# Modulation products in fewer, larger groups, and their loads spread over three parts of a step

## What is computed

```python
mod = jax.nn.silu(c) @ p['w_ada'] + p['b_ada']          # (9 rows, 9*2048)
sh1, sc1, g1, sh2, sc2, g2, sh3, sc3, g3 = jnp.split(mod, 9, axis=-1)
h = modulate(rmsnorm(x, p['g_ffn1']), sh1, sc1)
x = x + 0.5 * g1[:, None, :] * swiglu(h, p['w_up1'], p['w_down1'])
h = modulate(rmsnorm(x, p['g_mix']), sh2, sc2)
o, new_state = hybrid_mixer(h, ...)
x = x + g2[:, None, :] * o
h = modulate(rmsnorm(x, p['g_ffn2']), sh3, sc3)
x = x + 0.5 * g3[:, None, :] * swiglu(h, p['w_up2'], p['w_down2'])
```

## Time and profile before

| | |
|---|---|
| median of 3 runs | 2197.51 us (2195.69 to 2198.03) |
| the profiled execution's own time | 2197.48 us |
| its span, first to last instruction | 2195.7 us |
| TensorE matmul busy | 2130.8 us, 97% |
| VectorE, ScalarE, GpSimd busy | 55%, 39%, 6% |
| mean DMA rate | 243 GB/s |

### The profile page before, as it was taken

The page is one execution under the profiler, slowest core; times in us unless marked ns, Lnnn a source line. Parts: engine busy times, 40 slices in busy tenths (PEclk is TensorE's granted clock), DMA queues, the critical chain, the costliest instruction groups (busy, mean ns, idle before and its releaser), DMA issues.

```text
span 2195.7 us, 39972 instructions
## 1 busy us (share of the span) xinstructions
PE 2130.8 (97%) x17405; PEld 1975.2 (90%) x17405; DVE 1209.7 (55%) x1664; ACT 856.9 (39%) x1050; POOL 123.6 (6%) x146
## 2 busy tenths in 40 slices
PE   5999999999999999999988999999999999999998
PEld 4888879888989899989988998999999999999998
DVE  4355575444444445577788967444444444445555
ACT  3433333333333333356646534333433333333332
POOL 0000000000000000011675000000000000000000
PEclk9999999999999999999999999999999999999999
DMA  9988885988888887747554574866577777755453
GB/s 356 336 296 296 281 319 201 329 283 294 306 310 306 310 298 277 248 152 216 159 156 147 173 261 146 292 238 211 178 247 275 278 258 259 258 173 172 147 175 115
DMA packets 394270, 534.17 MB, mean 243 GB/s; under 512 B 13032, under 2 KB 358000, under 8 KB 375408
## 3 DMA queue, kind: packets, MB, share of 16 engines
q1 hardware_dynamic: 371792, 519.28, 68.5%
q10 hardware_dynamic: 22303, 12.33, 1.9%
HBM read 524.37 MB, written 7.19 MB: 242 GB/s over the span
## 4 chain that ended last, share of the span: by engine, by line
PE 88%; DVE 7%; DMA 2%; ACT 2%; issue 1%; SPq 1%; ACTq 0%; DVEq 0%
PE main L1631 23%; PE main L1632 22%; PE main L1633 22%; PE b L1554 5%; PE main L1697 4%; PE main L1699 4%; PE main L1698 4%; DVE w_lo L988 2%; PE b L1564 1%; DMA ada<-in_w_ada 1%; PE b L1577 1%; DMA first<-in_w_ada 1%; DVE ntile L1081 1%; SPq L525 1%; ACT w_hi L677 1%
## 5 line engine op out<-in xcount | busy, mean ns | idle before, releaser
L988 DVE TENSOR_TENSOR w_lo<-raw,w_hi 128x1024 fp32r<-128x1024 f32 (+2 forms) x720 | 796.3, 1113 | 890.8 <-ACT w_hi L677 889.4
L677 ACT ACTIVATE w_hi<-raw 128x1024 fp32r<-128x1024 f32 (+2 forms) x720 | 685.1, 956 | 1075.3 <-PE main L1633 914.1
L1631 PE MATMUL main<-h_hi,w_hi 128*128 128x264 f32 x2960 | 853.2, 288 | 13.5 <-DVE w_lo L988 4.5
L1632 PE MATMUL main<-h_lo,w_hi 128*128 128x264 f32 x2960 | 844.2, 285 | 0.0
L1633 PE MATMUL main<-h_hi,w_lo 128*128 128x264 f32 x2960 | 842.9, 285 | 0.0
L1631 PEld LDWEIGHTS main<-h_hi,w_hi 128*128 128x128 f32 x2960 | 559.9, 189 | 40.6 <-issue 17.8
L1632 PEld LDWEIGHTS main<-h_lo,w_hi 128*128 128x128 f32 x2960 | 558.8, 189 | 0.5
L1633 PEld LDWEIGHTS main<-h_hi,w_lo 128*128 128x128 f32 x2960 | 558.3, 189 | 0.0
L1631 PE MATMUL main<-act_hi,w_hi 128*128 128x264 f32 x1408 | 403.1, 286 | 0.0
L1633 PE MATMUL main<-act_hi,w_lo 128*128 128x264 f32 x1408 | 400.4, 284 | 0.0
L1632 PE MATMUL main<-act_lo,w_hi 128*128 128x264 f32 x1408 | 399.9, 284 | 0.0
(11 more groups left out here) (271 smaller groups left out, 996.0 us busy)
## 6 DMA issues: line engine op xcount, KB each, us to landing
raw<-in_w_up SPq DMA_DIRECT2D x132, 1024.0 KB, 5.3
ada<-in_w_ada SPq DMA_DIRECT2D x112, 1024.0 KB, 9.0
raw<-in_w_down SPq DMA_DIRECT2D x96, 768.0 KB, 5.0
raw<-in_w_up SPq DMA_DIRECT2D x88, 512.0 KB, 5.2
raw<-in_w_in SPq DMA_DIRECT2D x36, 1024.0 KB, 5.3
ada<-in_w_ada_f SPq DMA_DIRECT2D x32, 1024.0 KB, 9.0
ada<-in_w_ada SPq DMA_DIRECT2D x56, 512.0 KB, 7.7
raw<-in_w_down SPq DMA_DIRECT2D x32, 512.0 KB, 8.1
```

Source lines behind the costliest of these rows:

```text
L677: A(split_view(w_hi, m, kind), raw_piece(m, kind), ACT.Copy).then_inc(hi_done, 1)
L988: TT(split_view(w_lo, m, kind), raw_piece(m, kind), split_view(w_hi, m, kind).bitcast(F32), ALU.subtract).then_inc(lo_done, 1)
L1631: MM(out, wh, hi[:, k, :], start=k == 0, stop=False)
L1632: MM(out, wh, lo[:, k, :], start=False, stop=False)
```

## The change

Three things are changed. The products are issued in fewer groups: in the units, two behind every other unit and three behind the last unit of a quarter (`group_at`), and from step 11 on always four, at every other step or, from step 16 to 29, at every step. The loads of a step are issued not all behind part 2 but behind parts 0, 1, 1 and 2, except in the mixer. `mod_place` stands ahead of the piece work of part 3, not behind it. With this, `G1` is copied, turned and placed two units later.

```diff
-        for at, counts in ((UPS, (3, 3, 3, 3, 2, 2, 2, 2)), (UPS + DNS, (4,) * UPS), (2 * UPS + DNS, (2,) * 6),
-                           (S_FF2 + 2, (2,) * 6), (S_FF2 + UPS, (2,) * DNS), (S_FF2 + UPS + DNS, (2,) * 8)):
-            for n, count in enumerate(counts):
-                per_step[at + n] = count
+        for at, every, groups in ((UPS + 1, 2, 2), (UPS + DNS - 3, 1, UPS + 3), (2 * UPS + DNS, 2, 3),
+                                  (S_FF2 + 2, 2, 3), (S_FF2 + UPS, 2, 4), (S_FF2 + UPS + DNS, 2, 4)):
+            for n in range(groups):
+                per_step[at + every * n] = 4
...
+        group_at = {UPS * q + i: range(UPS * q + i - 1, UPS * q + i + 1) for q in range(QS) for i in (1, 3, 5, 7)}
+        group_at.update({UPS * q + 10: range(UPS * q + 8, UPS * q + 11) for q in range(QS - 1)})
+        group_at.update({38: range(37, 39), 40: range(39, 40)})
...
-                            if j == 2:
-                                for a in loads_at.get(s, ()):
-                                    if a == G3 * KD:
-                                        sp.wait_ge(h_ready, 3 * KD)
-                                        sp.wait_ge(stored, 16 * (len(OUT_COPIES) + 1))
-                                    ada_load(a)
+                            for a in loads_at.get(s, ()):
+                                if j != (2 if s >= S_XBC and s < S_FF2 else (0, 1, 1, 2)[a % 4]):
+                                    continue
+                                if a == G3 * KD:
+                                    sp.wait_ge(h_ready, 3 * KD)
+                                    sp.wait_ge(stored, 16 * (len(OUT_COPIES) + 1))
+                                ada_load(a)
...
-                if u == 40:
+                if u == 42:
                     ada_copy(G1)
...
-                if u == 41:
+                if u == 43:
                     mod_place(G1)
...
-                            pieces_ahead(s, j, PIECE_KIND[kind], follows)
                             if j == 3 and s in vec_ends:
                                 mod_place(vec_ends[s])
+                            pieces_ahead(s, j, PIECE_KIND[kind], follows)
...
-                if u == 40:
+                if u == 42:
                     ada_turn(G1)
...
-                if u < 40:
-                    stream_product(u)
+                for n in group_at.get(u, ()):
+                    stream_product(n)
```

More of the change, by code:

```diff
@@ L372, in stream @@
             return (q + 1, i) if i < 8 else (None, 3 * q + i - 8)
+        group_at = {UPS * q + i: range(UPS * q + i - 1, UPS * q + i + 1) for q in range(QS) for i in (1, 3, 5, 7)}
+        group_at.update({UPS * q + 10: range(UPS * q + 8, UPS * q + 11) for q in range(QS - 1)})
+        group_at.update({38: range(37, 39), 40: range(39, 40)})
+        assert [n for u in sorted(group_at) for n in group_at[u]] == list(range(40))
         slot_landed, stream_landed = [32] * 4, []
```

## The result

The changed kernel takes 2185.52 us (median of 5 runs, 2184.51 to 2187.82) against 2197.51 for the kernel before on the same chip: ratio 0.9947, with a 95% interval from 0.9934 to 0.9960. That is 12.0 us, 0.55% less; 2185.6 was forecast. The profiled execution took 2185.31 us, its span is 2183.6 instead of 2195.7.

The account below looks back on a forecast made before the run. TensorE, with matmuls busy 2130.8 of 2195.7 us, was taken as the bound, so only interruptions between weight pieces count. 12.5 - 8.1 + 4.6 + 2.9 = 11.9 us off 2197.5 gave 2185.6 us, range 2179 to 2191.5.

Parts of the forecast that it names:

- Part 1, fewer groups: Behind units and from step 11 on: 38 fewer groups of products, each saving a fixed 0.33 us, 12.5 us gained.
- the open bound: Quarter products in a row: slope 0.86 us taken; if nothing is shared, 1.19, the gain is 4.0 us less.
- Part 2, the cover that goes: Quarters 1 to 3: units without a product wait 0.51 us for VectorE's add to `acc_g`; 8.1 us lost in all.
- Part 3, the queue: SyncE's queue near unit 42: step 11's loads no longer hold up product 39's load, 4.6 us gained.
- Part 4, `mod_place`: First products of a vector: `mod_place` earlier ends waits of 1.02 and 1.50 us and two smaller, 2.9 us gained.
- Part 5, the loads: Dense down steps 16 to 18: last loads have 12.4 us to land, so no loss, 0 us.
- The other end of 2 us: Upper bound given for the loss from late loads in down steps 16 to 18, where 0 was taken.
- The rival that it would come out slower: Steps 17 to 19: loads come late, each late group costs up to 4.6 us, 2199.4 to 2204 us; chance 0.07.
- the wait that the prediction worked out from that limit: Steps 16 to 18 at 358 GB/s: last load 3.5 us late, one wait of 1 to 2 us, about 2187 us.
- the cover isn't missed: Units without a product lose nothing, 8.1 us more saved, 2177.5 us; chance 0.14.
- it is missed twice: Units without a product lose twice as much, or quarter products don't merge, 2189.6 to 2197.7 us; chance 0.22.
- part 3 merely moves: No-change rival: the queue stall reappears elsewhere at about 4.4 us, 2197 us; chance 0.07.

Follow-up runs that it names:

- experiment 7: The changed kernel with each group of four products in steps 19 to 29 split into two and two: 2188.51 us, ratio 0.9956.
- experiment 5: The changed kernel with VectorE's add to `acc_g` ahead of its unit's second `w_lo` piece instead of behind both: 2178.82 us, ratio 0.9913.
- experiments 5 and 6: The second of the two: the kernel before, with the add to `acc_g` ahead of its unit's second `w_lo` piece: 2198.24 us, ratio 0.9997.
- Experiment 1: The kernel before, with the loads for step 11 issued in step 11's own turn, not unit 42's: 2193.41 us, ratio 0.9980.
- Experiment 2: The kernel before, with `mod_place` ahead of the piece work of part 3 and nothing else: 2194.30 us, ratio 0.9985.
- experiment 4: The changed kernel with all loads of a step behind part 2 again, as before: 2200.47 us, ratio 1.0013.

## Why the prediction was right

**Part 1, fewer groups: 12.5.** It holds, in mechanism and size. In up steps a group less is worth 0.27 to 0.29 us (experiment 7; 0.81 for three in the second feed-forward part, 281.91 against 281.10). In down steps it is 0.34 (1.02 for three in steps 30 to 37, 1.37 for four in the second part). Behind units it is 0.33: units 3 and 4 together take 13.67 instead of 13.99, and units 14 and 15 take 14.11 before and 13.77 in the kernel of experiment 5, which has no waits there. With 21 groups behind units, ten in down steps and seven in up steps this makes 7.0 + 3.4 + 1.9 = 12.3. That quarter products merge was the open bound; the pair at 53.94 settles it.

**Part 2, the cover that goes: -8.1.** The waits are where they were put, 13 units at 0.50 us. Units 19 and 30 lose 0.28 each beyond the 0.22 of their transposes, and units 21 and 32 lose 0.52 and 0.55 by `acc_u`. For the whole, experiment 5 took 7.64 us, of which 0.6 behind units 40 and 41 was there before, and left 0.83 in units 21 and 32, where the kernel before had small stalls of 0.24 in all: 7.64 - 0.6 + 0.83 - 0.24 = 7.6. So the term is 0.5 too large. That what costs is the add's place in VectorE's order, once nothing covers it, is shown by experiments 5 and 6 together: the edit is worth 6.7 us or nothing, as the cover is gone or not.

**Part 3, the queue: 4.6.** Experiment 1 measured 4.64 in its stretch.

**Part 4, `mod_place`: 2.9.** Experiment 2 gained 2.8 by the steps in which the waits stood (1.07, 1.57 and twice 0.1), and 3.6 by the medians.

**Part 5, the loads: 0.** The number is right, the reasoning was thinner than it looked. It leant on 12.4 us for the last load, against a median of 10.1 and a largest landing of 14.4 that came from loads issued together. The measured times are 11.9 to 12.3 us from issue to product and 9.5 to 10.7 to land: no wait, with a margin of 1.2 us at the least. The other end of 2 us would have been too small for any real lateness: in experiment 4, where the last loads took 3.2 to 4.3 us longer to land, the price was 15 us. The rival that it would come out slower had its mechanism, place and nearly its price right (13.8 us for three late groups), and fell only through "they are now spread", which the prediction named as the evidence against and gave no number. The page DMA: Bandwidth & Descriptors of the Trainium skill, section Bandwidth, would have put the limit at about 358 GB/s. The 372 GB/s that passed over 80 us disagree, and the wait that the prediction worked out from that limit didn't come. The same section says that its measured figures are for one core alone, 425 GB/s for 16 MB, and that about 358 is what each of two cores gets when both stream; this kernel has one core, so the prediction took the figure that doesn't apply.

**The sum.** With what was measured it is 12.3 - 7.6 + 4.6 + 2.8 = 12.1, against 12.0 by the medians and 12.1 by the spans. Two small stalls of the kernel before, 0.2 at step 14 and 0.3 at step 19, went too. Against them stand three parts whose work was not changed: the opening up to the end of unit 0 (-0.3), the mixer (-1.0) and the final norm (+0.8). Over the nine profiles of this case the mixer takes 395.9 to 399.3 us, the end of unit 0 lies between 46.4 and 47.9, and the final norm takes 14.9 us in seven and 15.6 or 15.7 in two, whatever the kernel. So these differences are scatter. That the forecast was met to 0.1 us is partly chance, since the scatter is larger than that; that each part came out within 0.5 us of its term is not.

**The rivals.** That the cover isn't missed falls with the 14 waits; that it is missed twice with the 7.6; that part 3 merely moves with product 39's start at 330.68.

## What to carry to other kernels

When small work is gathered into larger groups, price both sides: the fixed part that is saved for each group, and what each of the old groups was hiding. Here the second side was over 60% of the first, and it was owed to one instruction that stood behind a wait it had no part in; moving that out of the way, which is worth nothing before the regrouping, made the regrouping pay more than half as much again. And when a group of work doubles, look at when its loads are issued among the others: here one condition in the queue's order decided between 12 us faster and 2.6 us slower.

## What was unexpected of the hardware

The time at the lower clock behind the same stall is not fixed. Product 39 waited 3.09 us in the kernel before and 3.12 us in that of experiment 2. Windows of these two, from 326 to 331 us, the first the row; here that of experiment 2:

```profile
326.00:331.00 5.00, 4.69 (x21) 3.02 (x22) 1.15 (x2) 0.00 (x0) 0.00 (x0) 0.50 1.06 341
```

The granted clock is 0.50 where it was 0.66. Behind the first weight matmul interval, 18 more are slower than 0.12 us, up to the 0.22 of the 1.2 GHz level, instead of 5, which is 1.3 us. At the first unit such a spell held 12 intervals in the kernel before and 25 in the changed one; over all nine profiles it is 12 in five and 22 to 26 in four, whatever the kernel. The Trainium skill says of the start of a kernel that the same kernel shows different numbers of slow matmuls from run to run (page TensorE: Matmul & The Clock Gate, section Part 1); these traces agree, and show it behind a stall in the middle too. So a stall of 3 us cost its length, 0.9 in the slow product behind it, and 0.6 to 1.9 in the weight matmuls after that. The parts above whose work is the same differ by up to 3.4 us between two single profiles, while a stretch without such a stall repeats to 0.01 us (steps 30 to 37 take 140.18 or 140.19 us in all five profiles with the new groups). So compare single profiles by such stretches, and not by their spans. And the DMA engines kept up 372 GB/s over 80 us in the changed kernel, with TensorE never waiting.
